# Order of the norm chains around the first block's output projection, in a one-core kernel of three blocks

## What is computed

```python
def first_block(x, ...):
    h = rmsnorm(x, mix_pre_norm)
    u = h @ w_in                      # u_a, u_b, hq, hk, hv, hg: 512 columns each
    y_conv = conformer_conv(u_a, u_b, ...)
    y_ret = retention_group(hq, hk, hv, hg)
    y = jnp.concatenate([y_conv, y_ret], axis=-1) @ w_out
    x = x + rmsnorm(y, mix_post_norm)
    h = rmsnorm(x, ffn_pre_norm)
    f = (silu(h @ w_ffn_gate) * (h @ w_ffn_up)) @ w_ffn_down
    ...
# conformer_conv: u_a * sigmoid(u_b), causal depthwise convolution of width 31,
#                 layernorm over the 512 channels, silu
# retention_group: rotary on q and k, 4 heads of 128, decayed scores (no softmax), times v,
#                 rms norm per head, times silu(hg)
```

## Time and profile before

| | us |
|---|---|
| median of three executions | 1450.79 |
| lowest and highest | 1449.22 and 1453.85 |
| the profiled execution, its own time | 1449.08 |
| its span, first to last instruction | 1447.2 |
| PE busy in the span | 1399.8 (97%) |
| POOL, DVE, ACT busy | 841.2, 710.7, 606.9 |
| mean granted clock of TensorE | 0.984 of 2.4 GHz |

### The profile page before, as it was taken

How to read it: one execution, slowest core, us unless ns; L and a number is a source line. 1 busy time by engine, 2 the same in 40 slices (tenths; PEclk the granted TensorE clock), 3 DMA queues, 4 the chain that set the end, 5 groups by cost and what they waited for, 6 DMA issues and landing times.

```text
span 1447.2 us, 25804 instructions
## 1 busy us (share of the span) xinstructions
PE 1399.8 (97%) x9145; PEld 1252.9 (87%) x9145; DVE 710.7 (49%) x1324; ACT 606.9 (42%) x973; POOL 841.2 (58%) x420
## 2 busy tenths in 40 slices
PE   9988999999999999799999999999999999999998
PEld 8988999999888888587888888888888788999997
DVE  5986555555724555836665565333424384311111
ACT  5454544544524445534332332322331265444452
POOL 5835788797464776152444444544365453688895
PEclk9998999999999999999999999999999999999999
DMA  7735477785332223031655555544293101455563
GB/s 263 249 123 204 155 275 276 283 302 182 124 100 76 71 66 99 1 117 59 214 192 201 186 193 197 195 167 153 78 252 109 44 14 62 143 181 181 179 211 105
DMA packets 82971, 227.27 MB, mean 157 GB/s; under 512 B 23648, under 2 KB 29024, under 8 KB 82656
## 3 DMA queue, kind: packets, MB, share of 16 engines
q1 hardware_dynamic: 82464, 224.91, 45.8%
q10 hardware_dynamic: 448, 1.57, 0.5%
HBM read 222.26 MB, written 1.05 MB: 154 GB/s over the span
## 4 chain that ended last, share of the span: by engine, by line
issue 36%; PE 29%; POOL 28%; DVE 4%; ACT 2%; DMA 1%; POOLq 1%; ACTq 0%; DVEq 0%; SPq 0%
POOL wl L544 25%; PE ps L1049 6%; PE ps L1050 6%; PE ps L1051 6%; PE ps L1136 1%; PE ps L1112 1%; PE ps L1113 1%; PE ps L1114 1%; PE ps L1383 1%; POOL xl L564 1%; PE ps L1309 1%; PE ps L1122 1%; PE ps L1330 1%; PE ps L1397 1%; PE ps L1375 1%
## 5 line engine op out<-in xcount | busy, mean ns | idle before, releaser
L544 POOL TENSOR_TENSOR wl<-raw,wh 128x1024 fp32r<-128x1024 f32 x310 | 743.3, 2418 | 540.9 <-ACT wh L634 540.8
L1049 PE MATMUL ps<-xh,wh 128*128 128x256 f32 (+1 forms) x1728 | 561.4, 325 | 11.0 <-DVE y L1626 4.6
L1050 PE MATMUL ps<-xl,wh 128*128 128x256 f32 (+1 forms) x1728 | 555.9, 322 | 0.0
L1051 PE MATMUL ps<-xh,wl 128*128 128x256 f32 (+1 forms) x1728 | 555.5, 321 | 0.0
L634 ACT ACTIVATE wh<-raw 128x1024 fp32r<-128x1024 f32 x310 | 318.6, 1053 | 291.8 <-PE ps L1051 206.7
L1049 PEld LDWEIGHTS ps<-xh,wh 128*128 128x128 f32 x1728 | 331.5, 192 | 43.1 <-issue 8.5
L1051 PEld LDWEIGHTS ps<-xh,wl 128*128 128x128 f32 x1728 | 331.2, 192 | 24.1
L1050 PEld LDWEIGHTS ps<-xl,wh 128*128 128x128 f32 x1728 | 331.5, 192 | 22.8
L1049 PE MATMUL ps<-fh,wh 128*128 128x256 f32 (+1 forms) x528 | 168.8, 320 | 1.7 <-POOL wl L544 1.7
L1051 PE MATMUL ps<-fh,wl 128*128 128x256 f32 (+1 forms) x528 | 168.6, 319 | 0.0
L1050 PE MATMUL ps<-fl,wh 128*128 128x256 f32 (+1 forms) x528 | 168.6, 319 | 0.0
(11 more groups left out here) (219 smaller groups left out, 1653.2 us busy)
## 6 DMA issues: line engine op xcount, KB each, us to landing
raw<-wall SPq DMA_DIRECT2D x310, 512.0 KB, 3.6
ada_late<-wada SPq DMA_DIRECT2D x56, 512.0 KB, 3.4
ada<-wada SPq DMA_DIRECT2D x40, 512.0 KB, 3.4
bias<-rpb SPq DMA_DIRECT2D x16, 256.0 KB, 6.2
h<-xin SPq DMA_DIRECT2D x2, 1024.0 KB, 7.2
sww<-qk SPq DMA_DIRECT2D x16, 128.0 KB, 2.3
csb<-cond SPq DMA_DIRECT2D x1, 1024.0 KB, 6.9
sw<-u ACTq DMA_DIRECT2D x2, 512.0 KB, 10.5
```

What stands on the lines that cost most here:

```text
L544: nc.gpsimd.tensor_tensor(wl[:, slot, :, :], raw[:, slot, :, :], wh[:, slot, :, :].bitcast(F32), ALU.subtract).then_inc(lo_ready, 1)
L1049: nc.tensor.matmul(o, wa, xa, start=start, stop=False, skip_group_check=True)
L1050: nc.tensor.matmul(o, wa, xb, start=False, stop=False, skip_group_check=True)
L1051: return nc.tensor.matmul(o, wb, xa, start=False, stop=stop, skip_group_check=True)
```

## The change

The convolution's and the retention's chains, the sums of the context's norm and the order in which `out` starts are rearranged; nothing of the result changes. The diff cut to its core:

```diff
-RET_BANKS = (0, 1, 3, 0)
+RET_BANKS = (0, 1, 0, 1)
-NORMS = ["pre1", "c0", "post1", "fpre1", ...]
+NORMS = ["pre1", "post1", "c0", "fpre1", ...]
+OUT = (1, 3, 0, 2, 4, 5, 6, 7)
+OUT_ROWS = ((0,), (1, 2), (3, 4), (5,))
# SP
-            sp.dma_start(dt_[:], ...)          # before unit 8
             sp.dma_start(rcs[:], ...)
-            stream(at_, at_ + SLOTS)
-            sp.dma_start(h[:, :, SEQ:NT], ...)
-            stream(at_ + SLOTS, 2 * PH["in_v"].step0)
-            for s in range(3):
-                load_ada("out", 0, s)
-            stream(2 * PH["in_v"].step0, 2 * PH["out"].step0)
+            for u_ in range(2 * PH["in_u"].steps, at_):
+                load(u_, u_ % SLOTS)
+                if u_ in (9, 10):              # half of the context each
+                    sp.dma_start(h[:, k:k + 4, SEQ:NT], ...)
+                if u_ == 12:
+                    sp.dma_start(dt_[:], ...)
+                if u_ in (14, 16, 18):
+                    load_ada("out", 0, u_ // 2 - 7)
             for u_ in range(2 * PH["out"].step0, at_):
-                load(u_, u_ % SLOTS)
-                if u_ >= at_ - 3:
-                    load_ada("out", 0, u_ - at_ + 6)
+                load(u_, u_ % SLOTS, 2 * PH["out"].step0 + OUT[u_ - 2 * PH["out"].step0])
+            for s in range(3, 6):
+                load_ada("out", 0, s)
# ACT: root("c0") moves from stream_summed("post1") to norm("fpre1"), behind the squares;
#      the Exp of lam moves from behind in_v to behind in_u
             act.wait_ge(S("ret_o"), 1)
             nc.scalar.activation(on[:], ret_ps..., ACT.Square)       # now ahead of
+            act.wait_ge(S("dev_ready"), 1)
+            nc.scalar.activation(sq[:, 0:4, 0:SEQ], cy[:], ACT.Square)  # this one
-            nc.scalar.activation(rstd[:, 0:SEQ], ps[:, 5, 0:SEQ], ACT.Sqrt, ...)
+            nc.scalar.activation(rcol[:, 0:2], ln_sums, ACT.Sqrt, ...)
             preload(ACT.Silu)
+            act.wait_ge(S("mix_ret"), 1)
+            for c in range(CONV_T, KT):        # moved ahead of the convolution's tiles
+                nc.scalar.activation(xh[:, c, 0:SEQ], mix[:, c, :], ACT.Copy)
             ...                                # silu and xh of tiles 0 to 3
-            second_step(PH["out"])
             condition_to(csb_ps)
+            second_step(PH["out"])
# PE
-            tokens(PH["in_v"], 2)              # then the mean into bank 2
+            tokens(PH["in_v"], 2, conv_mean)   # mean into bank 3, between pairs 0 and 1
+            keep_busy(8, 2)                    # behind scores times v
             pe.wait_ge(S("dev_sq"), 1)
-            4 x matmul(ps[:, 5, 0:SEQ], ones[:], sq[:, c, 0:SEQ])
+            8 x matmul(ln_sums[:, t:t + 1], sq[:, c, t * P:t * P + P], ones[:, 0:1])
-            keep_busy(14, 4)
+            keep_busy(8, 2)
             8 x transpose(...)                 # retained tiles, now into banks 3 and 4
-            norm_sum("c0", NT, SEQ)
-            keep_busy(12, 7)
-            features(PH["out"], SEQ, fresh=("xl_ready", KT, 1))
+            2 x transpose(ln_ps[:, t * P:t * P + P], rcol[:, t:t + 1].to_broadcast([P, P]), ident[:])
+            keep_busy(16, 7)
+            first_pairs()                      # units 24 to 27: tiles 4-7 for pairs 0 and 1, then 0-3
+            features(PH["out"], SEQ, first=1)  # units 28 to 31 as before
             norm_sum("post1", SEQ, waiting=(8, 3, 0))
             project_p(0)
-            norm_sum("fpre1", SEQ, waiting=(2, 3, 0))
+            norm_sum("c0", NT, SEQ)
+            norm_sum("fpre1", SEQ, waiting=(0, 0, 0))
# in norm_sum: keep_busy(20 if name == "fpre1" else 0, 1) is gone
# DVE
-                with dve.Fori(t0, t1) as t:                # one tap of two tiles per iteration
+                with dve.Fori(0, (t1 - t0) // 2) as t:     # two taps of two tiles per iteration
+                    tap(t * 2, t0)
+                    tap(t * 2, t0 + 1)
+                if (t1 - t0) % 2:
+                    tap(0, t1 - 1)
             # all four weighted(hd), then the deviation (before: three, deviation, the fourth)
-            link(V.reciprocal(rstd[:, 0:SEQ], rstd[:, 0:SEQ]))
+            V.reciprocal(rcol[:, 0:2], rcol[:, 0:2])
             # the retained tiles' gate (mix_ret) now ahead of cy * rstd; low parts in order 4-7, 0-3
-            recip("c0", NT, SEQ)               # ahead of take_summed
             take_summed(PH["out"], y, "post1") # condition rows per pair: 1, 2, 2, 1 (before 3, 0, 3, 0)
             recip("post1", SEQ)
             add_normed(y, par_ap("mix_post"))
+            recip("c0", NT, SEQ)
             recip("fpre1", SEQ)
```

More of the change, by code:

```diff
@@ L328, in pair_done @@
         def pair_done(eng, ph, i, pair):
-            eng.wait_ge(units_done, i * (2 * ph.body) + (2 * ph.step0 + 2 * ph.per_pair * (pair + 1) + SLOTS))
+            late = 1 if ph.name == "out" and pair == 0 else 0
+            eng.wait_ge(units_done, i * (2 * ph.body) + (2 * ph.step0 + 2 * ph.per_pair * (pair + 1) + late + SLOTS))
         def steps(eng, iters, per, depth, step):
@@ L720, in norm @@
                     nc.scalar.activation(sq[:, k, t0:n], src[:, k, t0:n], ACT.Square).then_inc(S("sq_ready"), 1)
+                if name == "fpre1":
+                    root("c0", NT, SEQ)
                 root(name, n, t0)
@@ L780, in _ @@
                 high_step(PH["in_u"], i, 1)
+            act.wait_ge(S("lam_dot"), 1)
+            nc.scalar.activation(lam4[:, 2:4], lam4[:, 0:2], ACT.Exp).then_inc(S("lam_exp"), 1)
             def take_qkg(i):
@@ L1075, in body, with tokens @@
                             mm.then_inc(units_done, 1)
-                run(pe, ph, body, ph.iters - 1 if within else 0)
-            def tokens(ph, tiles):
+                if first:
+                    body(1)
+                else:
+                    run(pe, ph, body, ph.iters - 1 if within else 0)
+            def tokens(ph, tiles, within):
                 def body(i):
                     for j in range(2):
+                        if j:
+                            within()
                         banks_ready(ph, i, j)
@@ L1150, in norm_sum @@
                 else:
-                    tiles = sum(KT for other in NORMS[:m] if other not in SUMMED)
-                    keep_busy(20 if name == "fpre1" else 0, 1)
+                    tiles = {"pre1": 0, "c0": KT, "fpre1": 2 * KT, "m0": 3 * KT}[name]
                     for k in range(KT):
@@ L1180, in _, with conv_mean @@
             features(PH["in_f"], SEQ)
-            tokens(PH["in_v"], 2)
[L1183 to L1187, removed]
+            def conv_mean():
+                pe.wait_ge(S("conv_tap"), CONV_T * CONV_W)
+                for c in range(CONV_T):
+                    mm = nc.tensor.matmul(ps[:, 3, 0:SEQ], ones[:], cy[:, c, :], start=c == 0, stop=c == CONV_T - 1)
+                mm.then_inc(S("ln_sum"), 1)
+            tokens(PH["in_v"], 2, conv_mean)
+            pe.wait_ge(bank_free, PH["out"].pair0 + 1)
             for hd in range(RET_H):
@@ L1198, in _ @@
                     .then_inc(S("ret_sc"), 1)
+            pe.wait_ge(bank_free, PH["out"].pair0 + 2)
             for hd in range(RET_H):
@@ L1524, in condition @@
                 both = csb_late if late else csb_ps
-                for s in range(per * j, per * j + per):
+                for s in rows or range(per * j, per * j + per):
                     dve.wait_ge(ada_landed[s % slots],
@@ L1743, in weighted @@
                 V.tensor_tensor(st[:, hd, :], ps[:, RET_BANKS[hd], 0:384], dt_[:, hd, :], ALU.mult).then_inc(S("ret_s"), 1)
-            for hd in range(3):
+            for hd in range(RET_H):
                 weighted(hd)
```

103 lines of the change are left out of this document (61 added, 42 removed).

## The result

Over 20 executions the changed kernel takes 1457.85 us in the median (1451.97 to 1462.52); the kernel before, 20 executions beside it, 1452.80 (1449.22 to 1456.62). The ratio is 1.0029, 95% interval 1.0019 to 1.0038: about 5 us slower. Forecast was 1449.0, with a range to 1454.5.

A forecast was written before the change was run, and what follows sets the result against it. PE, streaming weight units, was taken to set the pace outside the norms, so an earlier `gu` counts whole. 1449.08 - 6.3 + 4.6 = 1447.4 for the profiled execution; the median, 1.7 above, was forecast at 1449.0, range 1444 to 1454.5.

The forecast's parts named there:

- Stage a: Taps and weights' order, to `in_v`: taps end at 81.2 instead of 85.7, 4.5 us saved; values end 3.9 us earlier.
- rival 2: Taps of pass 1: they don't get faster, gain at `post1` only 1.8 us, 1453.5 us; chance 0.18.
- rival 3: Both passes of taps: DVE's sequencer becomes the bound, 5.3 us more than rival 2, 1458.8 us; chance 0.12.
- rival 4: Loads before `in_v`: their new order doesn't stop unit 21 being late, 1 to 2 us lost, 1450.5 us; chance 0.04.
- Stage b: Norms, from the retention's squares to the last `xh`: ends 0.3 us earlier, bounds -1 and +1.5.
- Stage c: `out`, first modulation row to `post1`'s last squares: DVE's chain takes 22.0 us instead of 23.8.
- Stage d: `c0` and `fpre1`: 64 column records in one run drop the clock inside it, 4.6 us lost (1.7 to 7.1).
- first term: The -6.3: `post1`'s last squares end at 135.1 instead of 141.4, 6.3 us earlier.
- Rival 1: Columns of `c0` and `fpre1`: the clock holds through them, 4.2 us less, 1444.8 us; chance 0.17.

The follow-up runs named there:

- x_c0_gap: Changed kernel with the 32 column records of `c0` and 20 fillers put between `out` and `post1`: 1448.47 us, ratio 0.9975 to the kernel before.
- y_rows: Kernel before with only the modulation rows split 1, 2, 2, 1 over the pairs and the late `ada` loads: 1455.67 us, ratio 1.0014.
- y_a_c_gap: Kernel before with stage a, the split rows, and `c0`'s columns with 20 fillers in the gap before `post1`: 1446.93 us, ratio 0.9952.
- x_back_gapfill: x_c0_back with 46 fillers in PE's idle time before `post1`: 1448.25 us, ratio 0.9964 to the kernel before.
- y_a_gap: y_a_c_gap with the rows in two blocks of three and their loads as before: 1452.2 us, ratio 0.9993 to the kernel before.
- y_c0_moved: Kernel before with only `c0` moved behind `pp` and the fillers of `fpre1` gone: 1458.06 us, ratio 1.0037.
- x_c0_back: Changed kernel with `c0` ahead of `out` again and the fillers of `fpre1` restored: 1451.67 us, ratio 0.9994 to the kernel before.
- x_fill_both: x_fill_cols with 46 more fillers in the idle time before `post1`: 1450.66 us, ratio 0.9991 to the kernel before.
- x_fill_cols: Changed kernel with two fillers behind every four column records of `c0` and `fpre1`: 1458.6 us, ratio 1.0033 to the kernel before.
- x_p_early: x_c0_gap with `ptf`'s read and `pth` moved ahead, rows (0, 1), (2), (3, 4), (5), 8 gap fillers: 1451.35 us, ratio 0.9983 to the kernel before.

## Why the prediction was wrong

- **Stage a held.** Taps at 82.4 against 81.2 (of it 0.84 the start), no wait for weights (the first goes with the order of loads, the second only with the mean between the pairs), PE's 0.76 before the mean against 0.3. The forecast took some 4 us from it, and alone it gave 4.75. Rivals 2, 3 and 4 are out; that the measured 1457.85 lies near rival 3's 1458.8 is chance, for the taps became faster. Not foreseen, since it was never asked: each of its parts alone gives nothing.
- **Stage b held where the clock did.** From the retention's squares to the end of the last `xh` 12.2 us were forecast; 12.14 in x_c0_gap (94.80 to 106.94), but 14.42 in the profiled changed kernel, with PE at half clock from 99.0 to 105.8. The wait for unit 26 was 2.49, "nearly 3". What was missed is `ptl`, 1.6 us, which the step left at its old duration though the work beside it had changed.
- **Stage c is the step that failed**: "PE's 4.55 of idle time and its half clock go too, but cover nothing more". DVE's chain was sized well, 22.5 us (118.35 to 140.84) against 22.0, and 21.5 in x_c0_gap, y_rows and y_a_c_gap. The text had both ends in hand, PE "done since about 130" and DVE at 135.1, and did not draw the conclusion: PE stands idle between them, immediately before the stage whose price is the clock. The idle time was not removed but moved. For the rows and late loads the sum had a gain, the part of 6.3 that was not stage a's 4.5; y_rows gives 2.9 lost. x_back_gapfill shows that filling the gap gives back 3.4, and y_a_c_gap beside y_a_gap that the split is then worth its 2.4.
- **Stage d was sized right for the wrong clock.** 4.6 lost was forecast (1.7 to 7.1), from a clock at full speed when the columns begin. (Twice the 3.63 us of the earlier trace rows is 7.3 and not 7.1; it changes nothing.) The kernel before, where it is at full speed, loses 4.9 (y_c0_moved). The changed kernel enters the columns at 1.2 GHz and loses 6.2. In the profiled execution gap and columns together cost 12.4 us from the squares' end to `gu`.
- In medians: forecast -6.3 + 4.6, measured -1.5 + 6.2 (x_c0_back against the kernel before, and the changed kernel against x_c0_back). Of the first term's 4.8 too much, 3.4 is the gap. The rest, 1.4, is less than such differences can tell; stage b's low clock and `ptl` are candidates, and no run splits it.
- Rival 1, the clock holding through the columns, is out, in both kernels. Of the rule that the prediction set beside it (the Trainium skill, TensorE: Matmul & The Clock Gate, Part 1, which ties the lower clock to an idle PE), the runs show both sides: idle time of 5.26 us is followed by 1.2 GHz and fillers in such idle time prevent that (x_fill_both, x_back_gapfill), as the page says; but y_c0_moved's clock falls among one-column matmuls with PE never idle. The prediction used the second against the first, where both held at once.

## What to carry to other kernels

When a change makes one engine finish earlier than the one it waits for, write down the idle time that this opens and what runs right behind it: here idle times of 4.4 to 5.3 us of TensorE before `post1` were paid again in the clock, with 4.4 to 5.1 us. Put work that must be done anyway into it (`c0`'s columns here, with fillers) and not behind it. A faster producer gains nothing while its consumer stands behind other work in its queue; the two belong to one edit.

## What the hardware showed that was not expected

- Fillers that compute nothing were worth 7.9 us (x_fill_both against x_fill_cols) and 3.4 us (x_back_gapfill against x_c0_back).
- Two fillers of 256 columns behind every four one-column records held the clock in the kernel before and in x_fill_both until 151.0, but not in x_fill_cols, at 152.1. One filler behind every four did not hold it in x_p_early, two or three did in x_c0_gap. The pattern of one stage alone does not tell what the clock will do.
- `ptl`, a DVE subtraction whose two inputs both lie in SBUF, takes 0.69 us with POOL idle and 2.19 to 2.32 with POOL at work; the rows, with one input in PSUM, keep 1.21 beside POOL. In the changed kernel it begins at 116.14 and ends at 118.43. POOL's second to fourth instruction of that stretch, each read by itself from its timeline:

```profile
115.50 2.38 POOL L550 TENSOR_TENSOR wl<-raw,wh 128x1024 fp32r<-128x1024 f32 x1
117.92 2.76 POOL L550 TENSOR_TENSOR wl<-raw,wh 128x1024 fp32r<-128x1024 f32 x1
120.63 2.41 POOL L550 TENSOR_TENSOR wl<-raw,wh 128x1024 fp32r<-128x1024 f32 x1
```

  `ptl` ends 0.55 after the instruction that it met (117.88), and 0.55 after it in each of the five other traces in which it met one. POOL's next instruction, begun before `ptl` was done, takes 2.76 in place of about 2.4. The Trainium skill, SBUF — State Buffer, SBUF: two separate sides, says that such a pair excludes one another for a whole instruction, and the later one is blocked. The trace agrees, both ways: of `ptl`'s own 0.69 all but 0.14 lies behind the end of POOL's instruction, and POOL's next is held in turn. The change had moved `ptl` from POOL's pause into its work, which the prediction did not look for.
- The granted clock and the time of single executions go together: 0.88 us per 0.001 in the changed kernel, 0.73 to 1.03 in the sets of 22 to 35 executions of the kernel before beside the experiments.
